# Memory heads' scores in two matmuls instead of three: the queries' high and low parts stacked on 128 rows

## The reference

```python
mkv = rms_norm(mem, mem_norm[l]) @ mem_w_kv[l]
km, vm = jnp.split(mkv, 2, axis=-1)
km = rms_norm(km.reshape(B, N_MEM, MEM_HEADS, MEM_HEAD_DIM), mem_k_norm[l])
vm = vm.reshape(B, N_MEM, MEM_HEADS, MEM_HEAD_DIM)
qm = rms_norm(memq.reshape(B, S, MEM_HEADS, MEM_HEAD_DIM), mem_q_norm[l])

def memory_attention(q, k, v):
    s = jnp.einsum('bqhd,bkhd->bhqk', q, k).astype(jnp.float32) * (MEM_HEAD_DIM ** -0.5)
    p = jax.nn.softmax(s, axis=-1)
    o = jnp.einsum('bhqk,bkhd->bqhd', p.astype(v.dtype), v)
    return o.reshape(B, S, MEM_HEADS * MEM_HEAD_DIM)
```

## Time and profile before

| | |
|---|---|
| median of 3 runs | 2188.93 us (2186.69 to 2193.8) |
| profiled execution | 2187.09 us, its span 2185.3 us |
| mean granted clock of PE | 0.989 |
| PE busy | 2131.3 us, 98% of the span |
| bytes moved | 370.64 MB |

### The profile page before, as it was taken

One profiled execution on the slowest core, in us unless ns is written; L12 is line 12 of the kernel. 1 busy time (PEld: TensorE's weight loads), 2 busy tenths in 40 slices (PEclk: granted clock), 3 DMA queues, 4 the chain that ended last, 5 costly groups with the idle time before them and its releaser, 6 DMA issues. The chain is left out here.

```text
span 2185.3 us, 31741 instructions
## 1 busy us (share of the span) xinstructions
PE 2131.3 (98%) x10024; PEld 1758.3 (80%) x10024; DVE 1429.2 (65%) x2097; ACT 1033.9 (47%) x1863; POOL 1094.8 (50%) x897
## 2 busy tenths in 40 slices
PE   8999999889999999989999999999999999999999
PEld 6899999767777777667888878888888888888887
DVE  5788888967666656477677787676734554354463
ACT  6566666557666666653333353333423233222221
POOL 2665566645465666558666666666446720020220
PEclk9999999989999999999999999999999999999999
DMA  6133233678567656665444554444567753233363
GB/s 242 38 112 92 81 98 119 176 221 257 183 183 220 196 176 190 209 216 169 150 158 159 197 203 159 158 158 160 187 241 279 241 204 106 98 136 138 137 222 116
DMA packets 291403, 370.64 MB, mean 170 GB/s; under 512 B 27280, under 2 KB 186192, under 8 KB 289488
## 3 DMA queue, kind: packets, MB, share of 16 engines
q1 hardware_dynamic: 291280, 369.08, 52.4%
HBM read 244.07 MB, written 124.93 MB: 169 GB/s over the span
## 5 line engine op out<-in xcount | busy, mean ns | idle before, releaser
L128 PE MATMUL bank<-f_t_hi,f_w_hi 128*128 128x512 f32 x896 | 350.9, 392 | 8.8 <-issue 4.3
L128 PE MATMUL bank<-f_t_hi,f_w_lo 128*128 128x512 f32 x896 | 350.1, 391 | 0.0
L128 PE MATMUL bank<-f_t_lo,f_w_hi 128*128 128x512 f32 x896 | 349.8, 390 | 0.0
L128 PE MATMUL bank<-f_w_lo,f_a_hi 128*128 128x512 f32 x896 | 348.5, 389 | 0.0
L128 PE MATMUL bank<-f_w_hi,f_a_hi 128*128 128x512 f32 x896 | 348.5, 389 | 0.0
L128 PE MATMUL bank<-f_w_hi,f_a_lo 128*128 128x512 f32 x896 | 348.5, 389 | 0.0
L2651 POOL TENSOR_TENSOR a_p_lo<-a_prob,a_p_hi 128x512 fp32r<-128x512 f32 (+1 forms) x192 | 233.9, 1230 | 177.7 <-DVE a_p_hi L2794 72.2
L128 PEld LDWEIGHTS bank<-f_t_hi,f_w_hi 128*128 128x128 f32 x896 | 169.0, 189 | 47.7 <-issue 8.4
L2088 DVE TENSOR_TENSOR f_a_lo<-f_a_raw,f_a_hi 128x1024 fp32r<-128x1024 f32 x112 | 158.9, 1419 | 71.7 <-ACT f_a_hi L2015 71.5
L1990 POOL TENSOR_TENSOR f_r<-f_r,f_y 128x512 f32<-128x512 f32 x24 | 41.6, 1766 | 325.1 <-DMA f_r<-s_x 325.1
L128 PEld LDWEIGHTS bank<-f_t_lo,f_w_hi 128*128 128x128 f32 x896 | 169.0, 189 | 35.1
(11 more groups left out here) (340 smaller groups left out, 4860.6 us busy)
## 6 DMA issues: line engine op xcount, KB each, us to landing
f_a_raw<-s_aop SPq DMA_DIRECT2D x112, 512.0 KB, 4.3
w_raw<-in_w_ff SPq DMA_DIRECT2D x64, 512.0 KB, 5.3
s_aop<-f_a SPq DMA_DIRECT2D x128, 256.0 KB, 4.4
s_aop<-f_s SPq DMA_DIRECT2D x96, 256.0 KB, 2.4
f_w_raw<-in_w_ff SPq DMA_DIRECT2D x64, 256.0 KB, 5.4
f_t_raw<-s_hop SPq DMA_DIRECT2D x14, 1024.0 KB, 8.8
f_r<-in_w_ff SPq DMA_DIRECT2D x48, 256.0 KB, 6.0
a_vals<-s_v SPq DMA_DIRECT2D x40, 264.0 KB, 4.8
```

What stands on the lines that cost most here:

```text
L128: ins = pe.matmul(out, a, b, start=(first and j == 0), stop=(last and j == n - 1))
```

## The change

The memory heads' scores take two matmuls. The queries' high and low parts lie on 128 rows of `q_lo` (high on 0 to 63, low on 64 to 127) and the keys' high part lies twice on 128 rows of `k_hi`, so that one matmul gives high by high plus low by high. The other matmul takes `k_lo` with `q_hi` over 65 rows: row 64 of `q_hi` holds the negated maximum, and row 64 of `k_lo` holds ones. For the latent heads there are still three matmuls; the maximum's row is row 96 and lies in one of them, the other two run over 96 rows. The `chunk` matmuls no longer read a row of zeros.

What goes with it: `k_mem` in DRAM holds two copies of the high part, and `k_mem_low` holds the low part with a row of ones, which DVE sets in the opening; `q_mem` interleaves the two heads of a pair by feature, so that one load takes both parts of a head, and `mem_q` is written in that order; POOL sets one constant row instead of five.

The core of the diff (the waits for the constant rows and the row numbers in the first loads are changed in the same way):

```diff
-    sb("kp_hi", [LD + 1, KP, CW])
-    sb("k_hi", [LD + 1, KR, CW])
+    sb("kp_hi", [LD, KP, CW])
+    sb("k_hi", [P, KR, CW])
     sb("k_lo", [LD + 1, KR, CW])
     sb("vals", [P, VR, CW // P, 2, VW])
     sb("q_hi", [LD + 1, RQ, UQ])
-    sb("q_lo", [LD + 1, RL, UQ])
+    sb("q_lo", [P, RL, UQ])
...
+def queries_low(S, x, h):
+
+    if x == "mem":
+        return S["q_mem"][:, :, h % 2, h // 2, :].rearrange("a d t -> (a d) t")
+    return S["q_mla"][1].rearrange("c p t -> (c p) t")[h * LD:(h + 1) * LD, :]
...
+def keys_high(S, x, h):
+
+    if x == "mem":
+        return S["k_mem"][:, :, h, :].rearrange("a d t -> (a d) t")
+    return S["k_mla"][0].rearrange("c p t -> (c p) t")[h * LD:(h + 1) * LD, :]
+
+
+def keys_low(S, x, h):
+
+    if x == "mem":
+        return S["k_mem_low"][:, h, :]
+    return S["k_mla"][1].rearrange("c p t -> (c p) t")[h * LD:(h + 1) * LD, :]
...
         sp.wait_ge(k_hi_done, NMT)
-        sp.dma_start(S["k_mem"][0, 0:MD], k_hi[:, :, :].bitcast(F32)).then_inc(stored, 16)
+        for copy in range(2):
+            sp.dma_start(S["k_mem"][copy], k_hi[:, :, :].bitcast(F32)).then_inc(stored, 16)
         sp.wait_ge(k_lo_done, NMT)
-        sp.dma_start(S["k_mem"][1, 0:MD], k_lo[:, :, :].bitcast(F32)).then_inc(stored, 16)
+        sp.wait_ge(ones_made, 3)
+        sp.dma_start(S["k_mem_low"], k_lo[:, :, :].bitcast(F32)).then_inc(stored, 16)
...
+        dve.memset(k_lo[MD:MD + 1, :, :].bitcast(F32), 1.0).then_inc(ones_made, 1)
...
-        mem_q = sb("mem_q", [P, MH, MD])
+        mem_q = sb("mem_q", [P, MP, MD, 2])
...
-                def constant_rows(n):
-                    name, value, done = (("kp_hi", 0.0, "k"), ("q_hi", 0.0, "q"), ("k_hi", 1.0, "k"), ("k_lo", 0.0, "q"), ("q_lo", 0.0, "q"))[n]
-                    pool.memset(R[name][0:1, :, :].bitcast(F32), value).then_inc(R[done + "_filled"], 1)
+                def constant_row():
+                    pool.memset(R["k_lo"][LD:LD + 1, :, :].bitcast(F32), 1.0).then_inc(R["k_filled"], 1)
+                    pool.wait_ge(R["k_filled"], 1)
...
-                row = q_hi[0:1, U % RQ, :].rearrange("a (q b i) -> a q b i", q=QT, i=TB)
+                D = units[U]["hd"]["D"]
+                row = q_hi[D:D + 1, U % RQ, :].rearrange("a (q b i) -> a q b i", q=QT, i=TB)
...
-            pe.matmul(pA[n % 2][:, 0:w], q_hi[0:D + 1, U % RQ, q * P:(q + 1) * P],
-                      kp_hi[0:D + 1, b, 0:w], start=True, stop=True).then_inc(scored, 1)
+            pe.matmul(pA[n % 2][:, 0:w], q_hi[0:D, U % RQ, q * P:(q + 1) * P],
+                      kp_hi[0:D, b, 0:w], start=True, stop=True).then_inc(scored, 1)
...
-                products(pe, pS[s % RS][:, c0:], [(kh[0:D + 1, keys], kl[0:D + 1, keys], qh[0:D + 1, c0:], ql[0:D + 1, c0:])]
-                         ).then_inc(qk_done, 1)
+                if units[U]["hd"]["causal"]:
+                    pe.matmul(pS[s % RS][:, c0:], kh[0:D, keys], qh[0:D, c0:], start=True, stop=False)
+                    pe.matmul(pS[s % RS][:, c0:], kl[0:D + 1, keys], qh[0:D + 1, c0:], start=False, stop=False)
+                    pe.matmul(pS[s % RS][:, c0:], kh[0:D, keys], ql[0:D, c0:], start=False, stop=True).then_inc(qk_done, 1)
+                else:
+                    pe.matmul(pS[s % RS][:, :], kl[0:D + 1, keys], qh[0:D + 1, :], start=True, stop=False)
+                    pe.matmul(pS[s % RS][:, :], kh[0:2 * D, keys], ql[0:2 * D, :], start=False, stop=True).then_inc(qk_done, 1)
...
-        q_mem=dram("q_mem", [2, 2, MD, MP, SEQ]), k_mem=dram("k_mem", [2, MD, MH, NMEM]),
+        q_mem=dram("q_mem", [2, MD, 2, MP, SEQ]), k_mem=dram("k_mem", [2, MD, MH, NMEM]), k_mem_low=dram("k_mem_low", [MD + 1, MH, NMEM]),
```

More of the change, by code:

```diff
@@ L170, in rings, with queries, keys_for_max @@
         R[f"front_{n}_stored"] = [ctx.enter_context(nc.semaphore(f"p_{n}_stored{b}")) for b in range(2)]
-    R["q_filled"], R["k_filled"] = (ctx.enter_context(nc.semaphore(f"a_{x}_filled")) for x in "qk")
+    R["k_filled"] = ctx.enter_context(nc.semaphore("a_k_filled"))
     return R
-def queries(S, x, part, h):
+def queries(S, x, h):
     if x == "mem":
-        return S["q_mem"][part, h % 2, :, h // 2, :]
-    return S["q_mla"][part].rearrange("c p t -> (c p) t")[h * LD:(h + 1) * LD, :]
-def keys_of(S, x, part, h):
+        return S["q_mem"][0, :, h % 2, h // 2, :]
+    return S["q_mla"][0].rearrange("c p t -> (c p) t")[h * LD:(h + 1) * LD, :]
+def queries_low(S, x, h):
     if x == "mem":
-        return S["k_mem"][part, :, h, :]
-    return S["k_mla"][part].rearrange("c p t -> (c p) t")[h * LD:(h + 1) * LD, :]
+        return S["q_mem"][:, :, h % 2, h // 2, :].rearrange("a d t -> (a d) t")
+    return S["q_mla"][1].rearrange("c p t -> (c p) t")[h * LD:(h + 1) * LD, :]
+def keys_for_max(S, x, h):
+    if x == "mem":
+        return S["k_mem"][0, :, h, :]
+    return S["k_mla"][0].rearrange("c p t -> (c p) t")[h * LD:(h + 1) * LD, :]
+def keys_high(S, x, h):
+    if x == "mem":
+        return S["k_mem"][:, :, h, :].rearrange("a d t -> (a d) t")
+    return S["k_mla"][0].rearrange("c p t -> (c p) t")[h * LD:(h + 1) * LD, :]
+def keys_low(S, x, h):
+    if x == "mem":
+        return S["k_mem_low"][:, h, :]
+    return S["k_mla"][1].rearrange("c p t -> (c p) t")[h * LD:(h + 1) * LD, :]
 def first_loads(sp, R, S):
@@ L321, in early_visits @@
                 first_highs=first_highs, first_lows=first_lows,
-                all_stored=all_stored, sems=sems, end=m_at)
+                all_stored=all_stored, m_low_made=m_low_made, sems=sems, end=m_at)
 def opening(nc, c, sb, sem, ident, A, S, W, x, x_loaded, at, xT_hi1, xT_lo1, banks):
@@ L343, in opening @@
     v_out = over("v_out", [P, MH, NMT, 2, VW], at["l_hi"], F32R)
-    k_hi, k_lo = (over(f"k_{n}", [MD, MH, NMEM], at["l_hi"] + (8 + 4 * b) * KB, F32R) for b, n in enumerate(("hi", "lo")))
+    k_hi, k_lo = (over(f"k_{n}", [MD + b, MH, NMEM], at["l_hi"] + (8 + 4 * b) * KB, F32R) for b, n in enumerate(("hi", "lo")))
     kn = [over(f"kn{b}", [P, MH, MD], at["mo"] + KB * b) for b in range(NMT)]
@@ L912, in drain @@
                     latent_gains(tc, l)
-                    for k in range(3, 5):
-                        constant_rows(k)
                 def body(i, s):
@@ L2560, in sync @@
                 sp.wait_ge(qk_done, end_of(U - RL))
-                sp.dma_start(q_lo[1:D + 1, b, :].bitcast(F32), queries(S, hd["x"], 1, hd["h"])[:, c_]).then_inc(ql_loaded[b], 16)
+                sp.dma_start(q_lo[0:D if hd["causal"] else 2 * D, b, :].bitcast(F32), queries_low(S, hd["x"], hd["h"])[:, c_]).then_inc(ql_loaded[b], 16)
             for n in of("k_load", s):
@@ L2565, in sync @@
                 sp.wait_ge(qk_done, piece_last[n - KR] + 1)
-                for e, k in enumerate((k_hi, k_lo)):
-                    sp.dma_start(k[1:hd["D"] + 1, b, 0:w].bitcast(F32), keys_of(S, hd["x"], e, hd["h"])[:, j * CW:j * CW + w]).then_inc(k_loaded[b], 16)
+                D, keys = hd["D"], slice(j * CW, j * CW + w)
+                sp.dma_start(k_hi[0:D if hd["causal"] else 2 * D, b, 0:w].bitcast(F32), keys_high(S, hd["x"], hd["h"])[:, keys]).then_inc(k_loaded[b], 16)
+                sp.dma_start(k_lo[0:D if hd["causal"] else D + 1, b, 0:w].bitcast(F32), keys_low(S, hd["x"], hd["h"])[:, keys]).then_inc(k_loaded[b], 16)
             for n in of("v_load", s):
```

43 lines of the change are left out of this document (21 added, 22 removed).

## The result

The changed kernel takes 2203.47 us (median of 4 runs, 2201.73 to 2205.17), the kernel before 2189.14 us beside it (4 runs, 2186.69 to 2193.8). The ratio is 1.0071, with a 95% interval of 1.0059 to 1.0082. The forecast was 2181.0 us and the range ended at 2187. The kernel is slower by 14 to 16 us, with 32 matmuls fewer. The profiled execution took 2204.63 us, with a span of 2202.9 and a mean clock of 0.988 (0.989 before).

What follows compares the result with a forecast made beforehand. PE, busy 98% of the span, sets the attention loop's pace. 7.4 for matmuls - 0.5 for waits + 0, with 0.1 for earlier exponentials, saves 7.0 us: profile 2180.1, median 2181.0 us, range 2177 to 2187.

Steps and rivals of the forecast that it cites:

- One shape is new: a score product over 128 rows in place of 65: Memory heads' score products: extra rows cost between 0 and 34 ns each, at most 1.1 us for 32; taken as 0.
- 7.4 us for 32 products: Attention loop: 32 of 96 memory-head score products go, worth 7.8 us by start-to-start distances, 7.4 after the lower clock.
- 131 ns a matmul: Skill's price per 512-column matmul in a sustained stream, 4.2 us for 32; rejected for the measured 0.233 us at full clock.
- In all I allow 0.5 us: Attention loop: loss to waits after shorter steps, bounds 0 and 7.9 us; DVE, ACT and POOL waits were expected to move along.
- rival 1: Attention loop: PE running ahead meets more waits, saving partly eaten, 3.5 us left, 2184.5 us; sign: idle up 2 us; chance 0.22.
- The transfers: Attention stage: 14 units fetch larger tiles, 2.7 MB more; hidden, as the tightest load is issued 11.5 us ahead.
- the opening: Added DVE memset of 1 x 1024 takes 0.9 us (bounds nothing and 2.22), swallowed by DVE's idle times.
- p_mem_q: Projection loop: DVE's interleaved write of the memory queries, 16 times, keeps its 0.41 us each; upper bound twice that, mostly hidden.
- rival 2: Attention stage: memory heads' low keys land late; from some 16 us landings slower by 0.3%, at 16.2 us 2196; chance 0.05.
- rival 3: Transitions (400 to 458, 908 to 953 us) fall better or worse by some 3 us: 2178 or 2184; chance 0.15.

Runs made afterwards that it cites:

- 65-row version: The changed kernel with the memory heads' maximum products back over 65 rows (a row of zeros) in place of 64: 2183.11 us, 0.9982 of before.
- the kernel before with one product less: The kernel before with the memory heads' product of high keys with low queries left out, 32 products fewer: 2182.83 us, 0.9980 of before.
- the extra product: The kernel before with one overwritten product ahead of each memory-head maximum product: 2192.76 us over 65 rows, 2219.97 over 64, 2221.02 over 48, 2220.93 over 32.

## Why the prediction was wrong

**The step that failed** is the sentence "One shape is new: a score product over 128 rows in place of 65", in the part on matmuls. More shapes are new. The diff also moves the maximum products of the memory heads from 65 rows to 64, and most products of the latent heads' scores from 97 rows to 96; the text ahead of the prediction says so ("The `chunk` matmuls no longer read a row of zeros"), and no term priced it. It looked like one row less of nothing. From 97 to 96 it was: the 65-row version has these too. From 65 to 64 it made 64 products of 64 rows stand in a stream in which all others have more, and cost 19.5 us (65-row version against the changed kernel), 0.30 us each. None of the rivals held it: the one on the other side was a late transfer, and the slower result was given 7 in 100. The 15.5 us (0.0071 x 2187) measured are these 19.5 less the 3.9 that the 65-row version saves; that sum closes by itself, since the same run stands in both terms. What bears it out are runs that share nothing with it: 4.4 us saved by the kernel before with one product less, and 27 us between 64 and 65 rows in the extra product.

Where the 19.5 us lie can be read from the two traces, though no run takes them apart. The stage is 22.0 us longer in the changed kernel; the rest of its span is 2.2 us shorter, as its stage began 2.4 us sooner. Set against the usual distance for each number of columns, the starts lie 17 us further apart at full clock and 7 us in the stretches at the lower clock (with the changes of rows that fall into them), and PE is idle for 2.2 us less. Between the extra products of 64 and of 65 rows the same three are 20, 9 and -1 us. That is how a change of rows can cost 0.38 us in the timelines, 0.42 in those runs and 0.30 here: the lower clock adds, and waits that the slower stream covers take away.

The Trainium skill has a rule that fits: its page "TensorEngine Tiling (Array Packing)", section "Tiling Modes", lists no row tiling for 128 rows and a twofold one for 64, and says that "Changing tiling mode (not just tile) drains the TensorE". The traces agree so far: the weight load isn't issued ahead on either side of the change. They don't show the mode itself, and 32 rows, for which the page has a third mode, cost the same as 64. The page gives no price; the runs here do.

**"7.4 us for 32 products"**: right as PE time. The distances in the 65-row version are 0.23 us for the step's first product and 0.24 for the second (medians of 0.2365 and 0.236, against 0.2305 to 0.235 before), so the rows up to 128 cost next to nothing, at most 0.4 us in sum. The 131 ns a matmul of the Trainium skill (page "TensorE: Matmul & The Clock Gate", section "Part 2: What happens when you issue a matmul"), weighed in the prediction, would have come to 4.2 us. That is nearly the time that was saved, but not for its reason: the distances are 0.23 us, and the measurement decides.

**"In all I allow 0.5 us" for the next waits** was mis-sized: they eat 3.0 to 3.5 us. The argument that the waits on DVE, ACT and POOL move along with PE doesn't hold: of the 2.8 us of new waits 2.3 are at DVE and ACT. That their work takes as long as before, and a PE that runs ahead meets it, is my reading; no run tests it. This was rival 1, with 3.5 us left of the saving and a chance of 0.22; its sign, an idle time longer by 2 us or more, is there, and the runs without the 64-row products land on it.

**The transfers, the opening and p_mem_q** came out as reckoned. PE waited for none of the 14 loads of the memory heads' low keys, issued 11.9 us or more before they were read; how long they took to land the trace of the changed kernel doesn't say. Its one wait for a_k_lo, 2.1 us for 1.0 before, is a latent head's. That isn't the layout: with the old one it is 1.0 to 2.1 us in the runs, with the new one 0.8 to 2.4. In the timeline of DVE in the changed kernel the memset took the estimated 0.9 us, and DVE still waited 2.47 us for ACT behind it (2.79 in the earlier trace rows):

```profile
34.92 0.91 DVE L492 MEMSET m_k_lo<- 1x1024 f32 x1 [0.27 <-issue]
...
41.03 1.23 DVE L1445 TENSOR_TENSOR p_xT_lo<-p_pG,p_xT_hi 128x1024 fp32r<-128x1024 f32 x1 [2.47 <-ACT p_xT_hi L1184]
```

The interleaved write is as fast as the plain one, against the earlier trace rows:

```profile
L1266 DVE TENSOR_TENSOR p_mem_q<-p_proj,p_stat x16: 409/414/2565, 57.9 to 405.5; 128x256 f32<-128x256 f32 x16
```

The late low keys (rival 2) and the transition (rival 3) did not show: the stage began at 452.9 us, for 453.2 before, and from its last score product to the end the kernel took 1276.4 us, for 1277.7.

## What to carry to other kernels

List every matmul whose shape a diff touches, also where it only drops a row, and ask of each whether it crosses 64 rows while its neighbours don't; a row of zeros may be what keeps the stream together. If products of up to 64 rows can't be avoided, put them side by side. And price what is taken off the bounding engine by its distance from start to start, then expect a tight loop to give back a part: here PE was 98% busy, and still over 40% of the first 32 products' time went into short waits, most of them on DVE and ACT. Look at the granted clock stage by stage even where its mean over the run is the same.

## What the runs showed of the hardware

- A change from more than 64 rows to 64, 48 or 32 and back costs about 0.38 us of TensorE at full clock in the timelines: some 0.09 us ahead, 0.19 behind, and 0.10 one further on. Several products of 64 rows in a row pay it once (0.13 us for each further one of 256 columns). Between 65, 96, 97 and 128 rows there is no such price.
- It shows in no wait on a semaphore and not in the share of busy time. It shows in the weight load's idle time ended by "issue" (21.4 us for 5.2), and in a mean length of 400 to 407 ns for 316 to 330.
- With such changes in the stream the granted clock fell to its lower level for 6.8 to 10.2 us in the middle of the stage, in six profiles of six; without them in none of six.
- The number of columns of the weights has no such price. In the first stage of the kernel before, at full clock, twelve times a product of 256 columns with 64 columns of weights stands behind one of 512 columns with 128 columns of weights: it starts 0.23 us behind it, and the way back takes 0.12 us.
- A product over 128 rows takes the same 0.23 to 0.24 us of the stream as one over 65.
